# Layer 1's gate products as seven half-size products, with modulation tiles placed anew

## What is computed

```python
def merge_branches(branches, gate_logits, w_branch, w_out):      # gate_logits = u @ w_in[:, gates]: (512, 1024) x (1024, 4096)
    gates = jax.nn.sigmoid(gate_logits)
    merged = gates[..., :D_MODEL] * (branches[0] @ w_branch[0])
    for i in range(1, N_BRANCH):
        merged = merged + gates[..., i * D_MODEL:(i + 1) * D_MODEL] * (branches[i] @ w_branch[i])
    return merged @ w_out

# modulation of each layer: six vectors of 1024 for the latent and six for the context tokens
m_lat = jax.nn.silu(c) @ w_mod + b_mod
m_ctx = jax.nn.silu(c_ctx) @ w_mod + b_mod
u_lat = h_lat * (1.0 + sc1) + sh1
```

## Time and profile before

| what | value |
|---|---|
| median of 3 runs | 2863.1 us (2861.0 to 2865.2) |
| the profiled execution's own time | 2864.5 us |
| its span in the profile | 2862.6 us |
| PE busy | 2722.6 us, 95% of the span |
| DVE busy | 1350.7 us, 47% |
| ACT busy | 436.0 us, 15% |
| POOL busy | 75.4 us, 3% |
| DMA | 239 GB/s as a mean, up to 421 in slices |
| granted TensorE clock | 0.998 of full speed |

### The profile page before, as it was taken

How to read it: one execution, slowest core, us unless ns; L and a number is a source line. 1 busy time by engine, 2 the same in 40 slices (tenths; PEclk the granted TensorE clock), 3 DMA queues, 4 the chain that set the end, 5 groups by cost and what they waited for, 6 DMA issues and landing times.

```text
span 2862.6 us, 42389 instructions
## 1 busy us (share of the span) xinstructions
PE 2722.6 (95%) x17586; PEld 1977.2 (69%) x17586; DVE 1350.7 (47%) x2753; ACT 436.0 (15%) x873; POOL 75.4 (3%) x137
## 2 busy tenths in 40 slices
PE   7999999998899899999988998899999999999998
PEld 3544444576666567788644444488788998988997
DVE  3856656442222233785411111179734764843763
ACT  0222220210000012231100000011422211122110
POOL 0100002000000000000100000000000000000000
PEclk9999999999999999999999999999999999999999
DMA  9623339379999985233899999954232444333441
GB/s 377 202 103 122 122 128 356 121 317 421 420 407 421 421 348 165 100 115 148 331 421 421 420 384 421 421 203 160 100 134 104 175 163 147 135 140 116 162 162 45
DMA packets 114765, 685.48 MB, mean 239 GB/s; under 512 B 20752, under 2 KB 22032, under 8 KB 39712
## 3 DMA queue, kind: packets, MB, share of 16 engines
q1 hardware_dynamic: 84144, 600.79, 53.1%
q0 software_dynamic: 16992, 69.54, 6.7%
q10 hardware_dynamic: 13456, 12.59, 1.7%
HBM read 679.46 MB, written 3.41 MB: 239 GB/s over the span
## 4 chain that ended last, share of the span: by engine, by line
PE 37%; DMA 14%; DVE 1%; issue 0%; ACT 0%; SPq 0%; DVEq 0%; ACTq 0%
PE ps L780 14%; DMA ring<-units 14%; PE ps L752 11%; PE ps L1527 2%; PE ps L1346 2%; PE ps L1222 2%; PE ps L1488 1%; DMA early_values<-arena 1%; PE ps L1358 0%; PE ps L1378 0%; PE ps L1088 0%; PE ps L815 0%; PE ps L789 0%; PE ps L798 0%; PE ps L1276 0%
## 5 line engine op out<-in xcount | busy, mean ns | idle before, releaser
L1222 PE MATMUL ps<-ring,arena 128*32 128x256 f32 x2928 | 359.8, 382 | 45.9 <-DMA ring<-units 44.4
L1207 PE MATMUL ps<-ring,arena 128*64 128x256 f32 x2960 | 339.3, 381 | 45.3 <-DMA ring<-units 45.1
L1207 PEld LDWEIGHTS ps<-ring,arena 128*64 128x64 f32 x2960 | 227.0, 137 | 148.7 <-issue 65.5
L1222 PEld LDWEIGHTS ps<-ring,arena 128*32 128x32 f32 x2928 | 175.2, 109 | 222.5 <-DMA ring<-units 90.9
L752 PE MATMUL ps<-h,ring 128*128 128x256 f32 (+1 forms) x992 | 246.0, 408 | 3.2 <-ACT h L1706 2.1
L1047 PE MATMUL ps<-u,ring 128*128 128x512 f32 (+1 forms) x544 | 235.1, 586 | 0.5 <-DVE arena L2345 0.5
L752 PEld LDWEIGHTS ps<-h,ring 128*128 128x128 f32 x992 | 186.7, 190 | 61.3 <-issue 34.7
L1047 PEld LDWEIGHTS ps<-u,ring 128*128 128x128 f32 x544 | 102.6, 191 | 126.7 <-issue 125.1
L2681 DVE COPY u<-ps 32x512 f32<-32x512 f32 (+1 forms) x128 | 70.9, 554 | 209.9 <-PE ps L1222 116.9
L752 PE MATMUL ps<-arena,ring 128*128 128x256 f32 x640 | 139.5, 379 | 1.3 <-DVE arena L3115 1.3
L752 PEld LDWEIGHTS ps<-arena,ring 128*128 128x128 f32 x640 | 121.4, 190 | 18.1 <-DVE arena L3008 1.7
(11 more groups left out here) (501 smaller groups left out, 3958.3 us busy)
## 6 DMA issues: line engine op xcount, KB each, us to landing
ring<-units SPq DMA_DIRECT2D x568, 1024.0 KB, 13.4
slots<-turned_mod POOLq DMA_DIRECT2D x62, 512.0 KB, 5.2
arena<-turned_mod POOLq DMA_DIRECT2D x18, 512.0 KB, 11.2
arena<-quarters ACTq DMA_DIRECT2D x32, 256.0 KB, 2.9
arena<-units POOLq DMA_DIRECT2D x7, 1024.0 KB, 7.2
h<-tokens SPq DMA_DIRECT2D x4, 512.0 KB, 12.2
arena<-neighbours ACTq DMA_DIRECT2D x32, 64.0 KB, 8.8
arena<-tokens ACTq DMA_DIRECT2D x1, 2048.0 KB, 14.2
```

The source lines that it names most:

```text
L1207: last = nc.tensor.matmul(ps[j * slots:(j + 1) * slots, bank, lo:lo + UC], lhsT[:, kt, 0:slots], row_of(w[j], kt), start=(kt == 0), stop=( ...
L1222: last = nc.tensor.matmul(ps[j % 4 * slots:(j % 4 + 1) * slots, banks[j // 4], 0:UC], lhsT[:, kt, 0:slots], row_of(w[j], kt), start=(kt == ...
```

## The change

**Layer 1's gate products of chunks 1 to 15** become seven products of half size in place of eight. The 1024 inputs, the 256 gate columns and the 512 tokens are each cut in two; a product is four matmuls of 128x128 by 128x256. DVE makes four sums of weight blocks for each chunk, one chunk ahead, and four sums of token blocks once, and adds the seven products up (`early_blocks`, `add_fifth`, `late_blocks`). The tanh is now taken of the summed gates in SBUF, in one instruction, and ACT copies the first product out of PSUM. Products go to the banks `gb`, `gb+1` and also `wb`, `wb+1`, so they wait for `merge` of the chunk before, and the branch product waits for the gates to be added.

**The ring** has four slots for the gate units and the units of `w_out`; the other four hold the sums. Units 36 to 39 are loaded when `mix_branches` has ended.

**Modulation tiles** are placed anew: 17 in `prepare` as before, 35 in the chunks, 15 after the last merge, and 13 in layer 2's `prepare` at three places. For the latter the latent conditions are stored to DRAM by POOL before its first tile, with a wait, and loaded again in layer 2, with seven slots for the tiles.

```diff
 HALF = S // 2 + 1
 MOD_SLOTS = 3
 MOD_BOTH = 48
+MOD_EARLY = 67
 MOD_TILES = 80
+AGAIN_SLOTS = 7
 MOD_LATE = 51
 
 
 def tile_places(early, late):
 
     used, last, places = {}, {}, []
-    for j in range(MOD_TILES):
+    for j in range(MOD_EARLY):
         s = j % early if j < MOD_LATE else (j - MOD_LATE) % (early + late)
         used[s] = used.get(s, 0) + 1
         places.append((s, used[s], last.get(s, -1)))
@@ -91,7 +93,15 @@
 
 TILE_PLACES = tile_places(MOD_SLOTS, 6)
 MOD_PREPARE = (2, 3, 4, 2, 2, 2, 2, 0, 0)
-MOD_MIX = (1,) + 10 * (3,) + (3, 10, 10, 9, 0)
+MOD_MIX = (1, 1, 3, 2, 1, 1, 3, 3, 1, 1, 3, 2, 3, 3, 3, 4)
+MOD_AGAIN = (0, 0, 0, 5, 0, 3, 0, 5, 0, 0)
+GATES, NARROW = 15, 35
+
+
+def slot_of(n):
+
+    return n % (RING // 2) if GATES < n < NARROW else n % RING
+
 
...
+        late_conditions = part(13824, 4, S)
+        again_slots = ([slots[:, s, :].rearrange("p (a n) -> p a n", n=S) for s in range(MOD_SLOTS)] +
+                       [h[:, 0:4, S:], h[:, 4:8, S:], branch[:, 0:4, S:], branch[:, 4:8, S:]])
         fmid = [part(12800, 2, 2 * S), part(13824, 2, 2 * S)]
         nsq = part(8704, 4, 512)
         rtmp = part(10752, 4, S)
 
+        wide_token_sums = [part(1024 * (i % 2), 4, S, of=ring[:, 4 + i // 2, :]) for i in range(4)]
+        wide_weight_sums = [[part(4 * P * i, 4, P, of=ring[:, 7 - q, :]) for i in range(4)] for q in range(2)]
+        gate_blocks = gate.rearrange("p j n -> p (j n)")
+        first_product_kept = small[:, 512:512 + S]
...
-            gaps = [2 * RING] + [n + RING for n in units_to_parks()] + [n_units]
+            for n in range(2 * RING, NARROW + 5):
+                if n < 2 * RING + RING // 2:
+                    sp.wait_ge(units_used, n - RING + 1)
+                elif n <= NARROW:
+                    sp.wait_ge(units_used, n - RING // 2 + 1)
+                else:
+                    sp.wait_ge(merged_step, 16)
+                sp.dma_start(ring[:, slot_of(n), :], units[n]).then_inc(loaded[n % RING], 16)
...
             pool.wait_ge(conditions_ready, 1)
-            modulation_tiles(0, MOD_LATE + MOD_SLOTS)
-            pool.wait_ge(mixed, 24)
-            modulation_tiles(MOD_LATE + MOD_SLOTS, MOD_TILES)
+            pool.dma_start(ap["late_conditions"], conditions[0][0:1, 0, :]).then_inc(conditions_stored, 16)
+            pool.wait_ge(conditions_stored, 16)
+            used = sum(MOD_PREPARE)
+            issued = used + MOD_SLOTS
+            modulation_tiles(0, issued)
+            for chunk in range(15):
+                used += MOD_MIX[chunk]
+                upto = min(used + (MOD_SLOTS if used < MOD_LATE else len(tile_slots)), MOD_EARLY)
+                if issued <= MOD_LATE + MOD_SLOTS < upto:
+                    pool.wait_ge(mixed, 24)
+                modulation_tiles(issued, upto)
+                issued = upto
+            modulation_tiles(issued, MOD_EARLY)
+            def again_tiles():
+
+                pool.wait_ge(u_ready, 2 * KT)
+                pool.wait_ge(bias_loaded, 16 * 16 * DEPTH)
+                pool.dma_start(late_conditions.rearrange("p a n -> p (a n)"), bass.AP(ap["late_conditions"].tensor, 0, [[0, P], [1, D]]))\
+                    .then_inc(conditions_loaded, 16)
+                for n in range(MOD_TILES - MOD_EARLY):
+                    if n >= AGAIN_SLOTS:
+                        pool.wait_ge(mod_taken, MOD_EARLY + n - AGAIN_SLOTS + 1)
+                    pool.dma_start(again_slots[n % AGAIN_SLOTS], ap["turned_mod"][MOD_EARLY + n].rearrange("p (a n) -> p a n", n=S))\
+                        .then_inc(again_loaded[n % AGAIN_SLOTS], 16)
+
             for l in range(DEPTH):
                 if l == 0:
-                    pool.wait_ge(mod_taken, MOD_TILES)
+                    pool.wait_ge(mod_taken, MOD_EARLY)
...
+                def gate_products(c):
+
+                    w = unit()
+                    s, t = wide_weight_sums[c % 2], wide_token_sums
+
+                    def product(bank, half, lhsT, rhs):
+                        for k in range(4):
+                            last = nc.tensor.matmul(ps[:, bank, half * S:(half + 1) * S], lhsT[:, k, :], rhs[:, k, :],
+                                                    start=(k == 0), stop=(k == 3))
+                        return last
+
+                    pe.wait_ge(gate_kept, 2 * c)
+                    product(gb + 1, 0, w[:, 0:4, 0:P], u[:, 0:4, 0:S]).then_inc(wide_first_ready, 1)
+                    product(gb, 0, w[:, 4:8, 0:P], u[:, 4:8, 0:S])
+                    pe.wait_ge(wide_tokens_summed, 1)
+                    pe.wait_ge(wide_weights_summed, c)
+                    product(gb, 1, s[1], t[1]).then_inc(wide_early_ready, 1)
+                    attend(2 * c)
+                    pe.wait_ge(merged_step, c)
+                    product(wb + 1, 1, s[0], t[0]).then_inc(wide_fifth_ready, 1)
+                    product(wb, 1, s[2], t[2])
+                    product(wb, 0, s[3], u[:, 4:8, S:]).then_inc(wide_late_ready, 1)
+                    pe.wait_ge(wide_fifth_added, c)
+                    product(wb + 1, 0, w[:, 4:8, P:UC], t[3]).then_inc(units_used, 1)
...
+                    elif l == 0:
+                        pe.wait_ge(gates_added, chunk)
...
+                    if l == 0 and chunk:
+                        exps(2 * chunk)
+                        act.wait_ge(wide_first_ready, chunk)
+                        A(first_product_kept, ps[:, gb + 1, 0:S], ACT.Copy).then_inc(wide_first_kept, 1)
+                        next_quarter(chunk)
+                        copies(2 * chunk)
+                        exps(2 * chunk + 1)
+                        copies(2 * chunk + 1)
+                        count.skip(units_used, 1)
+                        act.wait_ge(gates_added, chunk)
+                        A(gate[:, :, 0:T], gate[:, :, 0:T], ACT.Tanh, scale=0.5).then_inc(gate_kept, 2)
...
+                    if j < MOD_EARLY:
+                        s, times, before = TILE_PLACES[j]
+                        dve.wait_ge(mod_loaded[s], 16 * times)
+                        tile, by = tile_slots[s], modulated_tiles["from"][:, 0, :]
+                    else:
+                        times, s = (j - MOD_EARLY) // AGAIN_SLOTS + 1, (j - MOD_EARLY) % AGAIN_SLOTS
+                        dve.wait_ge(again_loaded[s], 16 * times)
+                        dve.wait_ge(conditions_loaded, 32)
...
+                    modulation_tiles((MOD_AGAIN if l else MOD_PREPARE)[place])
...
+                first, second, third, fourth = [gate_blocks[:, n * S:(n + 1) * S] for n in range(4)]
+
+                def first_wide_sums(c):
+                    n, to = GATES + c, wide_weight_sums[c % 2]
+                    w = ring[:, slot_of(n), :].rearrange("p (k c) -> p k c", c=UC)
+                    dve.wait_ge(loaded[n % RING], 16 * (n // RING + 1))
+                    dve.wait_ge(units_used, max(n - 1, GATES))
+                    v.tensor_tensor(to[0], w[:, 0:4, P:UC], w[:, 4:8, P:UC], ALU.add).then_inc(dve_step, 1)
+                    v.tensor_tensor(to[2], w[:, 0:4, 0:P], w[:, 0:4, P:UC], ALU.subtract)
+                    dve.wait_ge(dve_step, at(dve_step))
+
+                def last_wide_sums(c):
+                    n, to = GATES + c, wide_weight_sums[c % 2]
+                    w = ring[:, slot_of(n), :].rearrange("p (k c) -> p k c", c=UC)
+                    link(v.tensor_tensor(to[1], to[0], w[:, 0:4, 0:P], ALU.subtract))
+                    v.tensor_tensor(to[3], w[:, 4:8, 0:P], to[1], ALU.subtract).then_inc(wide_weights_summed, 1)
+
+                def early_blocks(chunk):
+                    dve.wait_ge(merged_step, chunk)
+                    dve.wait_ge(wide_first_kept, at(wide_first_kept))
+                    dve.wait_ge(wide_early_ready, at(wide_early_ready))
+                    link(v.tensor_tensor(gate[:, :, 0:S], ps[:, gb, :].rearrange("p (a n) -> p a n", n=S),
+                                         wide(first_product_kept, [P, 2, S]), ALU.add))
+
+                def add_fifth():
+                    dve.wait_ge(wide_fifth_ready, at(wide_fifth_ready))
+                    v.tensor_tensor(second, third, ps[:, wb + 1, S:], ALU.add).then_inc(wide_fifth_added, 1)
+
+                def late_blocks():
+                    dve.wait_ge(wide_fifth_added, at(wide_fifth_added))
+                    dve.wait_ge(wide_late_ready, at(wide_late_ready))
+                    link(v.tensor_tensor(gate_blocks[:, S:3 * S], gate_blocks[:, S:3 * S], ps[:, wb, :], ALU.add))
+                    dve.wait_ge(units_used, at(units_used))
+                    count.skip(units_used, -1)
+                    link(v.tensor_tensor(fourth, third, ps[:, wb + 1, S:], ALU.add))
+                    v.tensor_tensor(third, third, ps[:, wb + 1, 0:S], ALU.add).then_inc(gates_added, 1)
+
                 for chunk in range(16):
                     ahead = gate_units + chunk + 1, gate_weight_sums[(chunk + 1) % 2]
                     if l == 0:
```

(19 more changed lines are left out.)

54 lines of the change are left out of this document (32 added, 22 removed).

## The result

The changed kernel takes 2845.9 us (median of 5 runs, 2845.3 to 2848.6) where the kernel before takes 2863.1 (median of 5 as well): a ratio of 0.9944, with a 95% interval of 0.9930 to 0.9959. The forecast was 2844.0, within 2838 to 2855. The profiled execution spans 2844.1 us; the one before spanned 2862.6.

A forecast was written before the change was run, and what follows sets the result against it. PE was taken to bound layer 1's mixing: 24.6 + 2.2 - 4.4 - 1.0 - 0.9 = 20.5 us won, less 1.5 for the store, 19.0. From 2864.5 that gives 2845.5, median 1.4 lower: 2844.0 us, range 2838 to 2855.

The forecast's parts named there:

- PE's columns: Layer 1's gate products: 56 half-width records for 32 wide ones, winning 1.64 us a chunk, 24.6 us for 15 chunks.
- The estimate in cycles: Gate products by the skill's issue gaps, 56 x 262 against 32 x 518: 1.57 us a chunk, 23.6 us in all.
- DVE's chain in heavy chunks: Chunk 5's layout: VectorE's new sums and softmax are ready at 15.05 us, 0.2 us before PE needs them.
- The rival that this chain binds: Attention chunks: 0.1 us more per new VectorE step loses about 0.8 us a chunk in 11 chunks; 2850 to 2856, chance 0.12.
- The rival of a slower kernel: Same VectorE chain, much longer: eleven new instructions at 0.25 us more each lose 28 us, giving 2872; chance 0.07.
- The stall I counted for an overload ahead of chunk 8: With chunk 7's modulation tiles pushed into chunk 8, PE stalls 1.0 us in all.
- Chunks 12 to 15: Without attention between, the branch product waits 1.1 us a chunk for the gates to be added, costing 4.4 us.
- ACT's waits: PE's 4.3 us of waits on ACT's copies in the mixing: about half goes, 2.2 us won, bounds 0 and 4.3.
- the new small waits: Some five waits per chunk on PE, satisfied at once: 0.9 us lost, bounds 0 and 3.7 us.
- The store: POOL's 4 KB store before the first tiles takes 3.5 us; 1.5 us lost, bounds 0 and 10.
- The tail: After the last merge, 15 tiles and the first residual take DVE to 25.3 of 27.7 us: slack 2.4, cost 0, bounds 0 and 5.
- Layer 2: Its 13 tiles, 5, 3 and 5, fit DVE's idle times of 6.87, 3.89 and 7.59 us: cost 0, bounds 0 and 2.

The follow-up runs named there:

- the best spread: Changed kernel with later store, branch product's wait split, ring units held back, and modulation tiles spread anew (one less in chunks 6, 7, 12, 13): 2834.9 us, ratio 0.9903.
- the second trace: The changed kernel run once more with nothing changed, to see scatter: median 2845.8 us, ratio 0.9941 to the kernel before.
- the kernel with the split wait: Changed kernel, with the first half of the branch product waiting only for the sum that empties its bank: median 2847.8 us, ratio 0.9946 to the kernel before.

## Why the prediction was right, and where its terms were off

The mechanism was right: PE's columns decide, and VectorE has room if the tiles move. That the span came out within 0.5 us (18.5 us won for 19.0) is in part luck, for four misses nearly cancel: 1.35 us more in the mixing, 2.8 less at the store, 1.3 more from the shorter pause ahead of the first scores, which no term named, and 0.4 less behind. The median missed by 1.9 us, since 1.4 of it came from setting the profiled execution of the kernel before above its median; the changed kernel's profiled execution is its median.

**PE's columns: right.** 56 records at 0.216 us, 12.1 us a chunk; a chunk without attention or waits takes 15.52 us (12.10 plus the branch's 3.43), for 17.17 before. That is 1.65 us, for the 1.64 forecast. The estimate in cycles beside it doesn't follow as written: 56 x 262 against 32 x 518 is 1904 cycles, 0.79 us at 2.4 GHz. Only as a share (11.5%) of the measured 13.74 us does it give 1.58, near the 1.57 written; the forecast went by the rows.

**DVE's chain in heavy chunks: right.** Chunk 5 in the changed kernel starts at 254.69. The second softmax's product ends (its successor starts) at 269.63, 14.9 us in, for 15.05 laid out, and PE turns it at 270.08, 15.4 in, for 15.3. The late sums end at 271.2, 16.5 for 16.8. The rival that this chain binds, with a slack of 0.2 us only, did not come. The rival of a slower kernel speaks of eleven new VectorE instructions; its own list and the trace have nine. The stall I counted for an overload ahead of chunk 8 is 1.0 us in chunk 7 and 0.35 in chunk 8, for 1.0 in all.

**Chunks 12 to 15: under-sized.** I forecast 1.1 us each, 4.4 in all. Against the best spread (16.51 and three times 15.52) the changed kernel lost 5.8 us. The wait is 1.1 us by the trace, but 16.88 - 15.52 = 1.36 us by the chunk's length, and chunk 13 lost 0.3 us more. The four chunks together won only 0.6 us over the kernel before (68.85 for 69.45), where my terms give 1.9 (with four fifteenths of the small waits).

**ACT's waits: over-cautious.** 3.2 of the 4.3 us went by the table of waits, for the 2.2 taken. By the chunks' lengths it is more: chunks 1 to 11 won 21.25 us, of which the columns are 18.15, and with the stalls of 1.3 added back 4.4 are left, since gaps of 0.2 us that the table doesn't give to ACT went too. The price of the new small waits, 0.9 us, isn't to be seen: light chunks without a stall fell by 2.03 us (chunks 2 and 6, 22.01 to 19.98), more than the columns' 1.65. My terms give 18.6 for chunks 1 to 11. That and the last four chunks nearly cancel: 21.85 us in the mixing for 20.5.

**The store: the step that failed.** I took 3.5 us for its length, by its size of 4 KB, and it took 6.0, about midway between my bounds of 2.2 and 10.2 us. By these traces it is set by what is queued before it and not by its size: behind the three tiles the same 4 KB took 15.5 us to land, while the two stores of 512 KB that end the changed kernel, issued by SyncE with DMA idle until then (share 0.00), took 3.0 each. The 6.0 gave 2.8 us of wait for 1.5. And I left out what a wait of 4.6 us does to the clock behind it, another 1.5 (2.9 in the second trace). In all 4.4 to 6.0 us, for 1.5. The Trainium skill (DMA: Bandwidth & Descriptors, section Anatomy of one DMA), with 2.0 us fixed, was further off than my 3.5. Its warning of a long delay when the target is HBM isn't borne out as the cause here: the delay was long (5.7 us to landing), but a larger store to DRAM in an idle stretch landed in 3.0 us.

**The tail: right in its result, wrong in its slack.** PE didn't wait at the norm, as forecast, but not for the reason given. DMA held the last two tiles up by 3.4 us that I had set at 0, more than the 2.4 us of slack: the second residual starts at 497.73, 28.7 us behind the start of `w_out`, where the forecast needed 27.7. What saved it is a slack further on that I hadn't counted, between the folded sums and the matmul of the norm that takes them: 2.9 us in the kernel before (519.39 to 522.29), 1.9 in the changed one (501.48 to 503.40). I had called half of the DMA's 27 us harmless without looking which tile stands behind which unit. In the changed kernel this cost nothing; in the kernel with the split wait it took back what that had won.

**Layer 2: right.** Five, three and five tiles fit; PE's waits in that stage and just behind it (0.5, 0.9 and 1.0 us) are the same in both kernels. Behind it 0.4 us was lost (18.90 won at the experts' start, 18.5 at the end), which I can't tell from scatter.

## What to carry to other kernels

Move work onto another engine together with room for it: seven products alone made this kernel 4 us slower, freed room alone won nothing (and lost 4 by its store), both together won 17. Where an engine's queue overflows, the wait shows one stage behind the one with too much in it; take the work from the stage ahead (here a tile too many in chunk 6 showed in chunk 7, one in chunk 12 in chunk 13). A transfer on which the next requests wait should not stand in front of them while DMA is full. A wait of the bounding engine costs more than its length when the clock falls behind it, and a won microsecond must be followed to the next thing that is late.
